# Token and output projections of a two-layer hybrid trunk by three rounded products, with the weights' splits placed among other work, and the parameters in two transfers

## The chip, the cores and the metric

One core of a Trainium2 chip runs the whole program. The metric is the device time of one execution in microseconds, the median of several runs. The core's engines are TensorE (PE, matrix products; PEld is its weight load), VectorE (DVE), ScalarE (ACT), GpSimd (POOL) and SyncE (SP, which issues most transfers). Each has its own queue of instructions and they wait for each other by semaphores.

## The reference

One inference step through two layers, for 128 context tokens and 128 latent tokens of width 1024. Per layer:

```python
ada = silu(cond) @ ada_w + ada_b                 # six vectors of 1024
hm = rms_norm(x) * (1 + sc_m) + sh_m
a_qkv, a_z, a_dec, a_beta, r_qkv, r_g, n_qkv, s_bcx = split(hm @ w_in)
# gated delta rule | retention | neighbourhood attention | gated short convolution
x = x + g_m * (concat(o_gdn, o_ret, o_nat, o_sc) @ w_out)
hf = rms_norm(x) * (1 + sc_f) + sh_f
x = x + g_f * moe(hf)                            # 32 gated-MLP experts, top 1 group, top 2 experts in it
```

## The kernel before

Activations lie transposed: `hT` has 8 tiles of 128 features x 256 tokens (both groups of tokens side by side). The weights stream through a ring of four slots of 6144 columns each, filled by SyncE in a fixed order of loads (16 head slots and 32 experts per layer); a slot is refilled when a semaphore tells that its products are done.

A layer runs in these stages.

1. Opening. `ada` (L414) multiplies the ADA pieces 0 to 2 (load 0 to 2), `ada_rows` (L964, ScalarE) copies each row out, `ada_transpose` (L431, TensorE) turns it, `ada_columns` (L1219, VectorE) adds the bias to it. TensorE issues the transposition of piece i - 1 behind the products of piece i. `modulate` (L955 on ScalarE, L1229 on VectorE) then scales the normalised input.
2. Token projection (L462 to L473): the values of retention and attention and the gates of the delta rule, as plain float32 products, 16 of 512 columns and 16 of 16 columns. The profile shows a plain product as two matmul records.
3. Feature projection (L478): 12 units of 256 weight columns. Here each weight and each input is split into a high half, rounded to the type fp32r, and a low half, the difference; the product is high x high + high x low + low x high (L490, L491, L492). ScalarE makes the high half of a unit (`unit_high`, L979), VectorE the low half (`unit_low`, L1273) in place in the ring. The input's own halves are `ph_hi` (L977) and `h_lo` (L1271). VectorE's queue has the evacuation of the token products (L1253 to L1267) ahead of `h_lo` and of the first `unit_low`.
4. Attention, retention and delta rule. The delta rule runs two chunks (`s` = 0 and 1), each with an inversion by 7 levels (`b` = 0 to 6) for two directions (`g`): GpSimd masks a matrix (L1778), TensorE multiplies (L645), ScalarE copies (L1096), TensorE multiplies again (L666, L670), VectorE adds (L1472, L1474). In chunk 0 pieces of ADA products stand between the levels, in chunk 1 from level 1 on nothing. At the end the state's output (L695) is normed: ScalarE squares (L1100), TensorE sums (L706), ScalarE takes the root (L1103, L1105), VectorE multiplies (L1494, L1496).
5. Output projection (L713 to L726): 8 feature tiles x 8 inputs, 64 plain products of 256 columns, all behind the norm of the delta rule; the residual (L1503) and the sums of squares (L442) follow by parts.
6. Router and experts: 16 pairs, plain float32 products straight from the ring (L818, L867).

The parameters (`param`, 3003 columns: 955 of norms, biases, router and attention bias, then 2048 of cached keys, values and states) come by one transfer (L383), issued behind the layer's first four loads; in layer 1 it also waits until layer 0 is done. VectorE's first instruction of a layer waits for it (L1214, L1215).

## Time and profile before

| | us |
|---|---|
| median of three runs (lowest, highest) | 1288.18 (1279.51, 1291.25) |
| profiled execution | 1287.47 |
| its span | 1285.7 |
| TensorE busy in the span | 1102.2 (86%) |
| VectorE, ScalarE, GpSimd busy | 426.4, 273.8, 86.7 |

The span is what the profile's times refer to (microseconds from its start); the execution's own time has 1.8 us around it. Layer 0 ends near 653 us, layer 1 at the end. PEclk is the granted clock of TensorE as a share of its full speed. In a timeline a row has its start, its length, engine, line, operation, what it writes and reads, how often, and in brackets how long the engine was idle before it and who ended that. Lines are those of the kernel before.

### The profile page before, as it was taken

To read this page: it belongs to the slowest core of one execution; us is meant where nothing else is said; L and a number is where in the kernel's file an instruction comes from. 1 tells how busy PE (TensorE), PEld (TensorE's weight loads), DVE (VectorE), ACT (ScalarE), POOL (GpSimd) and SP (SyncE) were. 2 spreads that over 40 slices of the span, in tenths; PEclk is the share of its full clock that TensorE was granted. 3 is DMA by queue.
4 is the path that set the end of the run, shared out by engine and by line. 5 is a ranking of instruction groups with operands and counts; after the bars stand their busy time and mean duration, and the time that the engine had idled before them with its cause. 6 is when DMAs were issued, how large, how long until landed. Compare 5 with 4: busy or idle time off the path is not lost.

```text
span 1285.7 us, 18039 instructions
## 1 busy us (share of the span) xinstructions
PE 1102.2 (86%) x7588; PEld 781.2 (61%) x7588; DVE 426.4 (33%) x807; ACT 273.8 (21%) x426; POOL 86.7 (7%) x93
## 2 busy tenths in 40 slices
PE   4589877989867999999957996789888699999996
PEld 3379766979664444444354994678877544444443
DVE  0236544444133222222123555353531422222212
ACT  2224441111131111110023445111121211111100
POOL 0000112222000000000000002031310000000000
PEclk9789978999878999999978998799889699999998
DMA  9925630020162999999886256011106179999990
GB/s 391 406 98 197 256 117 34 19 86 2 73 253 97 420 395 412 411 414 410 358 348 281 105 197 263 12 34 38 67 1 253 74 291 407 405 411 413 413 405 36
DMA packets 24412, 299.02 MB, mean 233 GB/s; under 512 B 2944, under 2 KB 2944, under 8 KB 3200
## 3 DMA queue, kind: packets, MB, share of 16 engines
q1 hardware_dynamic: 23904, 296.67, 56.8%
q8 instruction: 66, 1.08, 0.3%
q0 software_dynamic: 416, 1.05, 0.3%
q14 instruction: 26, 0.21, 0.0%
HBM read 295.61 MB, written 2.10 MB: 232 GB/s over the span
## 4 chain that ended last, share of the span: by engine, by line
PE 77%; DVE 7%; issue 6%; ACT 4%; DMA 3%; POOL 1%; SPq 0%; DVEq 0%; POOLq 0%; ACTq 0%
PE ps L818 17%; PE ps L867 9%; PE ps L801 5%; PE ps L829 5%; PE ps L720 5%; PE ps L490 4%; PE ps L492 4%; PE ps L491 4%; PE ps L645 4%; PE ps L670 4%; PE ps L666 3%; DMA param<-in_param 3%; PE ps L466 2%; PE ps L426 2%; POOL arena L1778 1%
## 5 line engine op out<-in xcount | busy, mean ns | idle before, releaser
L818 PE MATMUL ps<-ring,arena 128*64 128x512 f32 x1024 | 226.8, 595 | 1.9 <-DVE arena L1631 1.9
L818 PEld LDWEIGHTS ps<-ring,arena 128*64 128x64 f32 x1024 | 71.6, 137 | 129.5 <-issue 129.1
L490 PE MATMUL ps<-arena_r 128*128 128x256 f32 x384 | 110.9, 289 | 10.4 <-DVE ring_r L1277 10.4
L867 PE MATMUL ps<-ring,arena 128*64 128x512 f32 x512 | 116.9, 598 | 2.0 <-DVE arena L1656 2.0
L492 PE MATMUL ps<-arena_r,ring_r 128*128 128x256 f32 x384 | 111.0, 289 | 0.0
L491 PE MATMUL ps<-hT_r,arena_r 128*128 128x256 f32 x384 | 109.1, 284 | 0.0
L1147 ACT ACTIVATE arena<-ps 128x256 f32<-128x256 f32 (+1 forms) x64 | 31.5, 492 | 244.9 <-PE ps L818 201.4
L426 PE MATMUL ps<-ring,condp 128*32 128x128 f32 x1536 | 57.3, 301 | 28.9 <-DMA ring<-in_ada_w 16.7
L490 PEld LDWEIGHTS ps<-arena_r 128*128 128x128 f32 x384 | 74.8, 195 | 10.6 <-DVE ring_r L1277 10.6
L1147 ACT ACTIVATE arena_r<-ps 128x1024 fp32r<-128x1024 f32 x32 | 32.8, 1024 | 205.9 <-PE ps L867 205.9
L829 PE MATMUL ps<-arena_r 128*128 128x256 f32 x512 | 71.8, 295 | 4.9 <-DVE arena_r L1642 4.9
L491 PEld LDWEIGHTS ps<-hT_r,arena_r 128*128 128x128 f32 x384 | 74.9, 195 | 0.0
L492 PEld LDWEIGHTS ps<-arena_r,ring_r 128*128 128x128 f32 x384 | 74.4, 194 | 0.0
L1277 DVE TENSOR_TENSOR ring_r<-ring,arena_r 128x2048 fp32r<-128x2048 f32 x24 | 54.8, 2291 | 59.1 <-ACT arena_r L987 58.9
L1652 DVE SCALAR_TENSOR_TENSOR arena<-ps,arena 128x256 f32<-128x256 f32 x32 | 15.5, 484 | 174.3 <-ACT arena L1147 174.3
L867 PEld LDWEIGHTS ps<-ring,arena 128*64 128x64 f32 x512 | 34.3, 136 | 60.8 <-issue 56.8
L829 PEld LDWEIGHTS ps<-arena_r 128*128 128x128 f32 x512 | 66.1, 199 | 6.7 <-DVE arena_r L1642 6.7
L1778 POOL TENSOR_TENSOR arena<-arena,const 128x512 f32<-128x512 f32 x56 | 60.5, 1096 | 131.8 <-PE ps L645 72.6
L720 PE MATMUL ps<-hT,ring 128*128 128x256 f32 x256 | 61.0, 403 | 8.5 <-DVE hT L1496 8.5
L426 PEld LDWEIGHTS ps<-ring,condp 128*32 128x32 f32 x1536 | 45.2, 120 | 36.2 <-issue 19.6
L801 PE MATMUL ps<-arena_r,param_r 128*128 128x512 f32 x128 | 56.3, 440 | 11.9 <-DVE hT_r L1668 11.9
L720 PEld LDWEIGHTS ps<-hT,ring 128*128 128x128 f32 x256 | 52.0, 204 | 18.1 <-DVE hT L1496 10.1
(293 smaller groups left out, 1486.8 us busy)
## 6 DMA issues: line engine op xcount, KB each, us to landing
ring<-in_moe SPq DMA_DIRECT2D x64, 2048.0 KB, 10.6
ring<-in_moe SPq DMA_DIRECT2D x64, 1024.0 KB, 10.6
ring<-in_ada_w SPq DMA_DIRECT2D x16, 3072.0 KB, 11.1
ring<-in_w_feat SPq DMA_DIRECT2D x8, 3072.0 KB, 14.0
ring<-in_w_tok SPq DMA_DIRECT2D x2, 2112.0 KB, 27.0
ring<-in_w_out SPq DMA_DIRECT2D x2, 2048.0 KB, 7.3
ring<-in_w_out SPq DMA_DIRECT2D x4, 1024.0 KB, 4.9
param<-in_param SPq DMA_DIRECT2D x2, 1501.5 KB, 25.5
```

The lines of the kernel that those rows point to most:

```text
L426: last = mm(ps[j:j + 32, bank_in, 0:P], condp[:, k, lead:lead + 32], slot[:, k * 768 + m * P:k * 768 + (m + 1) * P], start=u < 4, stop=u > ...
L490: mm(out, hi, ph_hi[:, k, :], start=k == 0, stop=False)
L491: mm(out, hi, h_lo[:, k, :], start=False, stop=False)
L492: last = mm(out, low[:, k, tile], ph_hi[:, k, :], start=False, stop=k == KT - 1)
L720: last = mm(ps[:, f // 2, (f % 2) * TOK:(f % 2 + 1) * TOK], slot[:, at:at + P], hT[:, k, :], start=k == 0, stop=k == KT - 1)
L801: last = mm(bank(bank_out), x[:, s, k * P:(k + 1) * P], sel_r[:, g % 2, s, :], start=n == 0, stop=n == 3)
L818: last = mm(ps[64 * i:64 * i + 64, q % 2, :].rearrange("p (w n) -> p w n", w=2), xg[:, g % 2, k, c0 + 64 * i:c0 + 64 * i + 64], weights[i] ...
L829: last = mm(ps[:, 4 + f // 2, (f % 2) * TOK:(f % 2 + 1) * TOK], y[:, f * P:(f + 1) * P], sel_t[:, q % 2, :], start=q == 0 and f % 2 == 0 a ...
L867: last = mm(ps[64 * i:64 * i + 64, 2 + half, :], act_t[:, q % 2, kk * P + 64 * i:kk * P + 64 * i + 64], ring[(2 * q + i) % RING][:, at:at ...
L1147: go(out, inp, how).then_inc(sem[name], 1)
L1277: tt(tiles768(ring_r[in_load(i) % RING][:], cols), tiles768(ring[in_load(i) % RING][:], cols), pw_hi[v % 2], ALU.subtract).then_inc(sem["p ...
L1778: G.tensor_tensor(group(g, 6), group(g, 2), bc(levels[:, g, b, :].unsqueeze(1), HEADS, P), ALU.mult)\
```

## The change

- The token weights are split as the features' are: ScalarE's high half behind the second ADA row, VectorE's low half behind the second ADA columns. The token weights are loaded ahead of ADA piece 2 for that. The projection is 96 rounded products: high x high in two halves, low x high, high x low.
- VectorE makes the input's low half and the first two units' low halves ahead of the evacuation of the token products.
- The output weights are split in four chunks of 256 columns. ScalarE makes the high halves in levels 2 to 4 of the second inversion and behind it, VectorE the low halves in levels 3 to 5 and behind it. The mixed outputs of retention, attention and convolution are split in levels 1 and 2, those of the delta rule behind its norm.
- The output projection is 192 rounded products. For the first six feature tiles, the products with inputs 2 to 7 stand ahead of the delta rule's norm, those with inputs 0 and 1 behind it; tiles 6 and 7 follow whole.
- The first 955 parameter columns are loaded behind the constants in layer 0, and for layer 1 among the experts of layer 0; the other 2048 stay where the single transfer was.

The diff, cut to its core:

```diff
+TOK_LOAD = 2
 def ada_load(i):
-    return i if i < ADA_FIRST else i + IN_SLOTS
+    return i if i < TOK_LOAD else i + 1 if i < ADA_FIRST else i + IN_SLOTS
 def in_load(i):
-    return ADA_FIRST + i
+    return ADA_FIRST + i if i else TOK_LOAD
...
+                        sp.dma_start(param[:, 0:CACHE], src["param"][l][:, 0:CACHE]).then_inc(sem["param_dma"], 16)
                     if i == RING - 1:
                         if l > 0:
                             sp.wait_ge(sem["layer_done"], l + 1)
-                        sp.dma_start(param[:], src["param"][l]).then_inc(sem["param_dma"], 16)
+                        sp.dma_start(param[:, CACHE:PARAM_W], src["param"][l][:, CACHE:PARAM_W]).then_inc(sem["cache_in"], 16)
                 for q in range(PAIRS):
+                    if q == 2 and l < DEPTH - 1:
+                        sp.wait_ge(sem["flag"], rise(l, "flag", 1))
+                        sp.wait_ge(sem["route_mm"], rise(l, "route_mm", 1))
+                        sp.dma_start(param[:, 0:CACHE], src["param"][l + 1][:, 0:CACHE]).then_inc(sem["param_dma"], 16)
...
+                pe.wait_ge(sem["t_hi"], rise(l, "t_hi", 1))
+                for half in range(2):
+                    pe.wait_ge(sem["h_hi"], rise(l, "h_hi", half + 1))
+                    for part in range(4):
+                        token_products(part, tok_high, ph_hi, True, False, range(4 * half, 4 * half + 4))
+                pe.wait_ge(sem["t_lo"], rise(l, "t_lo", 1))
+                for part in range(4):
+                    token_products(part, tok_low, ph_hi, False, False)
+                pe.wait_ge(sem["h_lo"], rise(l, "h_lo", 1))
+                for part in range(4):
+                    last = token_products(part, tok_high, h_lo, False, True)
...
-                for i, tiles in enumerate(OUT_TILES):
-                    in_slot(l, out_load(i))
-                    for m in range(tiles):
-                        for k in range(KT):
-                            last = mm(ps[:, f // 2, (f % 2) * TOK:(f % 2 + 1) * TOK], slot[:, at:at + P], hT[:, k, :], ...
+                def out_products(f, ks, start, stop):
+                    for n, k in enumerate(ks):
+                        mm(out, high_half(f // 2, k)[:, cols], pm_hi[:, MIX_AT[k], :], ...
+                        mm(out, high_half(f // 2, k)[:, cols], h_lo[:, k, :], ...
+                        last = mm(out, lo[:, k, cols], pm_hi[:, MIX_AT[k], :], ...
+                pe.wait_ge(sem["h_lo"], rise(l, "h_lo", 2))
+                for f in range(6):
+                    pe.wait_ge(sem["p_lo"], rise(l, "p_lo", f // 2 + 13))
+                    out_products(f, range(2, KT), True, False)
+                    if f == 0:
+                        pe.wait_ge(sem["gn_sq"], rise(l, "gn_sq", 1))
+                        mm(bank(7), C("blockones"), group(0, 3).rearrange("p h c -> p (h c)"), start=True, stop=True).then_inc(sem["gn_mm"], 1)
+                pe.wait_ge(sem["h_lo"], rise(l, "h_lo", 3))
+                for f in range(6):
+                    last = out_products(f, range(2), False, True)
+                    if f in (3, 5):
+                        last.then_inc(sem["out_mm"], 1)
+                pe.wait_ge(sem["p_lo"], rise(l, "p_lo", 16))
+                out_products(6, range(KT), True, True)
+                norm_sum(norm2, 2, 5, range(first[0], first[1]))
+                out_products(7, range(KT), True, True).then_inc(sem["out_mm"], 1)
...
                 ada_rows(0, 6)
                 inverse_rms(1)
-                for i in range(1, ADA_FIRST):
-                    ada_rows(i, 6 + i % 2)
+                ada_rows(1, 7)
+                for part, ks in enumerate((slice(0, TOK_K * TOKCOLS), slice(TOK_K * TOKCOLS, KT * TOKCOLS))):
+                    last = go(pt_hi[part].rearrange("p k n -> p (k n)"), ring[n % RING][:, ks], ACT.Copy)
+                last.then_inc(sem["t_hi"], 1)
+                ada_rows(2, 6)
                 modulate(1)
-                go(ph_hi, hT[:], ACT.Copy).then_inc(sem["h_hi"], 1)
+                go(ph_hi[:, 0:4, :], hT[:, 0:4, :], ACT.Copy).then_inc(sem["h_hi"], 1)
+                go(ph_hi[:, 4:KT, :], hT[:, 4:KT, :], ACT.Copy).then_inc(sem["h_hi"], 1)
...
+                        if s == 1 and b in (2, 3, 4):
+                            out_high(b - 2)
+                out_high(3)
...
-                        for i in range(ADA_FIRST):
+                        for i in range(2):
                             ada_columns(i, 5)
+                        dve.wait_ge(sem["t_hi"], rise(l, "t_hi", 1))
+                        for part, ks in enumerate((slice(0, TOK_K * TOKCOLS), slice(TOK_K * TOKCOLS, KT * TOKCOLS))):
+                            last = tt(ring_r[in_load(0) % RING][:, ks], ring[in_load(0) % RING][:, ks], pt_hi[part]..., ALU.subtract)
+                        last.then_inc(sem["t_lo"], 1)
+                        ada_columns(2, 5)
...
+                        if s == 1 and b == 2:
+                            tt(h_lo[:, 2:6, :], hT[:, 2:6, :], pm_hi[:, 0:4, :], ALU.subtract)
+                            tt(h_lo[:, 6:8, :], hT[:, 6:8, :], pm_hi[:, 6:8, :], ALU.subtract).then_inc(sem["h_lo"], 1)
+                        if s == 1 and b in (3, 4, 5):
+                            out_low(b - 3)
```

On VectorE, at the opening of a layer, the kernel before has this order (`adaT` holds the ADA columns, `scale` the modulation's factors):

```order
L1223 TENSOR_TENSOR adaT<-ps,param 128x12 [waits ada_tr]
L1221 REGISTER_ALU
L1223 TENSOR_TENSOR adaT<-ps,param 128x12 [waits ada_tr]
L1227 SCALAR_TENSOR_TENSOR scale<-adaT,param 128x16 [waits ada_dve]
L1243 ISA
L1248 TENSOR_SCALAR hT<-hT,scale,adaT 128x128 [waits h_scaled]
```

and the changed kernel this one, from the second of the three sums on:

```order
L1311 TENSOR_TENSOR adaT<-ps,param 128x12 [waits ada_tr]
L1327 TENSOR_TENSOR ring_r<-ring,arena_r 128x2640 [waits t_hi]
L1327 TENSOR_TENSOR ring_r<-ring,arena_r 128x1584
L1309 REGISTER_ALU
L1311 TENSOR_TENSOR adaT<-ps,param 128x12 [waits ada_tr]
L1315 SCALAR_TENSOR_TENSOR scale<-adaT,param 128x16 [waits ada_dve]
L1337 ISA
L1342 TENSOR_SCALAR hT<-hT,scale,adaT 128x128 [waits h_scaled]
```

The subtraction of the token weights, 2640 and 1584 columns, has moved in between the second and the third sum.

On TensorE, at the end of the delta rule, the kernel before goes from the state's output to the norm's sum and then to the output projection:

```order
L695 MATMUL ps<-arena,param 128x128 x2
L706 MATMUL ps<-arena,const 128x512 [waits gn_sq]
L720 MATMUL ps<-hT,ring 128x256 [waits sc_dve,slot_in1,nat_out,gn_out]
L720 MATMUL ps<-hT,ring 128x256 x31
L720 MATMUL ps<-hT,ring 128x256 [waits slot_in2]
```

In the changed kernel L742 is the state's output; 18 rounded products follow, of which the last three stand here, then the norm's sum (L774) and the next tile:

```order
L763 MATMUL ps<-param_r,arena_r 128x256
L764 MATMUL ps<-hT_r,arena_r 128x256
L765 MATMUL ps<-param_r,ring1_r 128x256
L774 MATMUL ps<-arena,const 128x512 [waits gn_sq]
L763 MATMUL ps<-param_r,arena_r 128x256 [waits p_lo]
```

The norm's sum has 18 products ahead of it, and 90 more stand between it and the first product that waits for the norm.

On VectorE, in the second inversion, an output chunk's low half stands behind the last update of a level (L1583) and ahead of the first of the next (L1581):

```order
L1581 TENSOR_TENSOR arena<-arena,ps 128x512 [waits inv_umm]
L1582 REGISTER_ALU
L1583 TENSOR_TENSOR arena<-arena,ps 128x512 [waits inv_umm]
L1522 REGISTER_ALU
L1525 TENSOR_TENSOR ring1_r<-ring1,arena_r 128x8x256 [waits p_hi]
L1578 REGISTER_ALU
L1580 REGISTER_ALU [waits inv_upd]
L1581 TENSOR_TENSOR arena<-arena,ps 128x512 [waits inv_umm]
```

Before, the same rows stand there without the two in the middle.

## Rows read from the trace of the kernel before

**Rows 1.** The chain that ended last, by engine, from the page

```profile
PE 77%; DVE 7%; issue 6%; ACT 4%; DMA 3%; POOL 1%; SPq 0%; DVEq 0%; POOLq 0%; ACTq 0%
```

**Rows 2.** Groups by line: shapes, count, busy us, mean ns, idle before and its releaser

```profile
L818 PE MATMUL ps<-ring,arena 128*64 128x512 f32 x1024 | 226.8, 595 | 1.9 <-DVE arena L1631 1.9
...
L490 PE MATMUL ps<-arena_r 128*128 128x256 f32 x384 | 110.9, 289 | 10.4 <-DVE ring_r L1277 10.4
...
L1277 DVE TENSOR_TENSOR ring_r<-ring,arena_r 128x2048 fp32r<-128x2048 f32 x24 | 54.8, 2291 | 59.1 <-ACT arena_r L987 58.9
...
L987 ACT ACTIVATE arena_r<-ring 128x2048 fp32r<-128x2048 f32 x24 | 45.6, 1907 | 3.8 <-PE ps L492 3.8
```

**Rows 3.** Stretches: us, busy (x) of PE, PEld, DVE, ACT, POOL, PEclk, DMA share, GB/s

```profile
30.00:44.00 14.00, 4.59 (x98) 4.25 (x97) 0.74 (x2) 0.28 (x1) 0.00 (x0) 0.78 1.01 430
...
76.00:82.00 6.00, 6.00 (x28) 6.00 (x29) 2.10 (x1) 0.00 (x0) 0.00 (x0) 0.50 0.60 258
...
90.00:140.00 50.00, 50.00 (x427) 50.00 (x426) 28.38 (x36) 23.80 (x19) 0.00 (x0) 1.00 0.49 190
...
282.00:292.00 10.00, 8.94 (x51) 8.75 (x52) 3.16 (x5) 1.19 (x2) 3.61 (x4) 0.66 0.45 188
```

**Rows 4.** Timeline of layer 0, opening and token projection

```profile
43.12 0.69 DVE L1215 TENSOR_TENSOR param<-param,const 128x512 f32<-128x512 f32 x1 [42.11 <-DMA param<-in_param]
...
48.12 0.17 DVE L1223 TENSOR_TENSOR adaT<-ps,param 128x12 f32<-128x12 f32 x1 [0.86 <-PE ps L435]
...
48.53 3.18 ACT L961 ACTIVATE hT<-hT,adaT,scale 128x128 f32<-128x128 f32 x8 [1.10 <-DVE scale L1227]
...
51.77 15.51 PE L466 MATMUL ps<-ring,hT 128*128 128x512 f32 x32 [3.69 <-ACT hT L961]
...
75.95 0.58 PE L490 MATMUL ps<-arena_r 128*128 128x256 f32 x1 [5.20 <-DVE ring_r L1277]
```

**Rows 5.** Timeline of layer 1, opening

```profile
659.85 5.35 PE L426 MATMUL ps<-ring,condp 128*32 128x128 f32 x96 [10.68 <-issue]
...
672.35 0.28 ACT L968 ACTIVATE adarow<-ps 128x128 f32<-128x128 f32 x1 [1.03 <-PE ps L435]
...
675.37 0.17 DVE L1223 TENSOR_TENSOR adaT<-ps,param 128x12 f32<-128x12 f32 x1 [1.64 <-PE ps L435]
...
676.60 3.18 ACT L961 ACTIVATE hT<-hT,adaT,scale 128x128 f32<-128x128 f32 x8 [0.90 <-DVE scale L1227]
```

**Rows 6.** Timeline of layer 0, levels 4 and 5 of the second inversion

```profile
302.90 1.95 PE L645 MATMUL ps<-arena 128*128 128x128 f32 x16
...
308.39 1.95 PE L645 MATMUL ps<-arena 128*128 128x128 f32 x16
...
305.91 0.69 DVE L1472 TENSOR_TENSOR arena<-arena,ps 128x512 f32<-128x512 f32 x1 [2.12 <-PE ps L666]
...
309.48 0.60 ACT L1096 ACTIVATE arena<-ps 128x512 f32<-128x512 f32 x1 [4.00 <-PE ps L645]
...
304.04 2.15 POOL L1778 TENSOR_TENSOR arena<-arena,const 128x512 f32<-128x512 f32 x2 [3.35 <-PE ps L645]
```

**Rows 7.** Timeline of VectorE and GpSimd ahead of the second inversion

```profile
276.54 1.16 DVE L1448 TENSOR_TENSOR arena<-arena 128x256 f32<-128x256 f32 x1
...
278.53 0.43 DVE L1448 TENSOR_TENSOR arena<-arena 128x256 f32<-128x256 f32 x1
...
276.33 1.09 POOL L1778 TENSOR_TENSOR arena<-arena,const 128x512 f32<-128x512 f32 x1 [0.70 <-DVE arena L1434]
```

**Rows 8.** Timeline of layer 0, end of the delta rule and output projection

```profile
322.55 0.61 PE L695 MATMUL ps<-arena,param 128*128 128x128 f32 x4
...
329.70 23.45 PE L720 MATMUL ps<-hT,ring 128*128 128x256 f32 x96 [4.24 <-DVE hT L1496]
...
354.72 7.07 PE L720 MATMUL ps<-hT,ring 128*128 128x256 f32 x32
...
328.95 0.69 DVE L1496 TENSOR_TENSOR hT<-arena 128x512 f32<-128x512 f32 x1
```

More of the change, by code:

```diff
@@ L122 @@
 GROUP_W = 8 * 512
+CACHE = PARAM["ck"].start
 PER = dict(
@@ L469, in _, with token_products @@
-                for s in range(NS):
-                    for k in range(KT):
-                        last = mm(ps[:, proj_bank(2), 16 * s:16 * s + 16], hT[:, k, s * P:(s + 1) * P],
-                                  slot[:, k * TOKCOLS:k * TOKCOLS + 16], start=k == 0, stop=k == KT - 1)
-                last.then_inc(sem["proj_mm"], 1)
+                def token_products(part, weight, x, start, stop, ks=range(KT)):
+                    out, cols = ((ps[:, proj_bank(part), 0:16 + TOK], slice(0, 16 + TOK)) if part < 2 else
+                                 (ps[:, proj_bank(2), (part - 2) * TOK:(part - 1) * TOK], slice(16 + TOK, TOKCOLS)))
+                    for k in ks:
+                        last = mm(out, x[:, k, part % 2 * P:(part % 2 + 1) * P], weight(k)[:, cols],
+                                  start=start and k == 0 and part < 3, stop=stop and k == KT - 1, skip_group_check=True)
+                    return last
@@ L1417, in _, with out_low @@
                 copy(qdec.rearrange("p d j (i n) -> p (d j i) n", i=2), bc(gdec[:, 1, :].unsqueeze(2), 8, HD)).then_inc(sem["qd_g"], 1)
+                def out_low(c):
+                    i, part = out_chunk(c)
+                    dve.wait_ge(sem["p_hi"], rise(l, "p_hi", c + 13))
+                    for k0, count, ap in po_hi[c]:
+                        ks = slice(k0, k0 + count)
+                        last = tt(part(ring_r[out_load(i) % RING])[:, ks], part(ring[out_load(i) % RING])[:, ks], ap, ALU.subtract)
+                    last.then_inc(sem["p_lo"], 1)
                 for s in range(NS):
```

138 lines of the change are left out of this document (91 added, 47 removed).

## Prediction

> **What bounds the kernel now.** I read the chain that ended last first, then the lines, then the timeline of the places that the change touches. TensorE makes up 77% of the chain [rows 1]; what it computes, at what clock, and what it waits for is the time. The largest part, the experts, is untouched: TensorE waits there 1.9 us in the whole run for VectorE and not at all for weights [rows 2]. So the gain has to come from the two head stages of each layer.
>
> The clock has to be read with it. A rounded product of 256 columns takes 6.00/28 = 214 ns where the granted clock is 0.50, and 50.00/427 = 117 ns where it is 1.00 [rows 3]. These are the levels of 1.2 and 2.4 GHz.
>
> First place, the token projection: 16 + 16 plain products run from 51.77 us, and only at 75.95 us does the first rounded product of the features start, after 5.20 us of idle time that VectorE's subtractions end [rows 4]. That is 24.2 us; layer 1 has the same two pieces. The idle time is all that L490 shows: 10.4 us in 384 products, 5.2 in each layer [rows 2]. After it the clock is at 0.50 for a window of 6 us, so 28 products cost 28 x (214 - 117) = 2.7 us more. Second place, the output projection: TensorE is done with the state at about 323.1 us (the last row of L695), waits for the norm of the delta rule until 329.70, and the last plain product ends at 361.8 us [rows 8].
>
> **The opening gets longer.** The token weights are now split before the third ADA piece is added up. On ScalarE that is a copy of 4,224 columns: L987 needs 1907 ns for 2048, so 3.93 us. On VectorE it is a subtraction of as many: 2291 ns for 2048, so 4.72 us [rows 2]. Both stand in their engine's queue between ADA piece 1 and ADA piece 2, and the modulation waits for piece 2. VectorE can't begin it early in layer 0, since it first adds piece 1, whose transposition TensorE issues behind the products of piece 2.
>
> Layer 0: VectorE begins at 43.12 us today, when the parameters, the last of the first transfers, have landed [rows 4]. At 430 GB/s [rows 3], the 2048 columns of caches and states (1.05 MB), now last, take 2.4 us, so piece 2 lands at 40.6 us instead of ahead of the token weights. Its 48 products take 5.35 us after a long idle time, as piece 0 does in layer 1 [rows 5], to 46.0; I give the transposition and the sum of piece 1 0.75 us, the subtraction 4.72, and from the sum of piece 2 to the modulation 48.53 - 48.12 = 0.41 [rows 4]. The modulation starts at 51.85 instead of 48.53: 3.3 us late. The shorter wait for parameters is more than used up.
>
> Layer 1: ScalarE copies row 1 at 672.35, and VectorE adds piece 1 at 675.37 [rows 5], so there the split's start is ScalarE's. Its end, 672.6, + 3.93 + 4.72 + gaps and 0.41 gives 681.8 instead of 676.60: 5.2 us late. The parameters landed late in layer 1 too, but what released the modulation there was the sum of piece 2. Together +8.5. The bounds of this term: 0, if the splits cost nothing, and 2 x (3.93 + 4.72) = 17.3, if nothing hides any of them.
>
> **Token products: 11.6 us less per layer.** Removed: 24.2 us and the 2.7 of the low clock. Added: a copy of half of the rounded input (1024 columns, about 1.0 us) before the first product, then 96 products. Half have 256 columns at 117 ns, half 272, in proportion 124 ns: 11.6 us. They now start after the longer idle time at the low clock; I charge the same 2.7 us. No row shows 272 columns; the nearest are 256. If a product of 272 cost nothing more, 0.3 us would go; if all 96 ran at 214 ns, 8.9 would come. Sum 15.3 against 26.9. No wait remains before the features: VectorE's subtraction of the input (2.29) and of the first two weight units (2.29 each) follow one another within 9 us of the modulation, under 14 us of products. What now stands behind these subtractions is the evacuation of the token products; ScalarE's gates wait for it, and behind them the third weight split. I get that split done about 0.8 us before TensorE asks, so it is at the edge; if it comes late, a microsecond or two per layer goes.
>
> **Output products: 13.5 us less per layer.** 192 rounded products at 117 ns are 22.5 us, against 329.70 to 361.8 = 32.1 now [rows 8]. More than half need nothing of the delta rule's norm: 6 feature tiles x 6 inputs x 3 = 108 products, 12.7 us, which fill the wait. From 323.1: 18 products (2.1), the norm's sum (512 plain columns, four pieces at 0.22, 0.9), 90 products (10.5), to 336.6. The norm's chain, ended at 329.6 by L1496 [rows 8], is moved back about 1 us by the first 18 products and gets a copy and a subtraction of 512 columns (a quarter of L987 and of L1277, 0.5 and 0.6): 331.7, so it is hidden by nearly 5 us. Then 36 products (4.2), 24 (2.8), the sum over four tiles (8 pieces at the 0.22 of L720's last row, 1.7 [rows 8]), 24 (2.8): 348.3 against 361.8. The engine comes here at full clock and doesn't stop. The residual and norm behind it are as before.
>
> The splits that make this possible lie in the levels of the second inversion. A level of 5.49 us leaves ScalarE 4.00 us free (copies of 1.9 us fit) and VectorE 2.12 us between the last update and the next level's first [rows 6]. A subtraction of 2.29 overruns by 0.2; an update has 0.2 of slack to the next, so this is made up. The third chunk, in three pieces, overruns by 0.45 at the last level, which nothing makes up: +0.9 in both layers. The fourth lies behind the evacuation of the state, where VectorE waits for the norm anyway.
>
> **A place where the levels can collide.** At 276.54 a VectorE operation with both inputs in SBUF took 1.16 us while GpSimd ran from 276.33 to 277.42; the same line took 0.43 at 278.53, with GpSimd idle [rows 7]. The updates, with one input in PSUM, keep their 0.69 beside GpSimd [rows 6]. The new subtractions are of the kind that was held up. They would start about 0.25 us ahead of GpSimd's pair of masks (304.04), so GpSimd waits some 2 us; its second mask would end near 308.2, and TensorE asks for the first at 308.39.
>
> The Trainium skill (SBUF — State Buffer, section Who interferes with whom) says that the port pair of the two engines is an exclusive lock and that issue order decides who blocks. The trace agrees (1.16 against 0.43 us); by that rule alone it is VectorE that goes first, and the sum above stands unless the order flips.
>
> **Sum.** +8.5 (opening) - 23.2 (token) - 27.0 (output) + 0.9 (levels) = -40.8 us. The profiled execution took 1287.47 us (span 1285.7), 0.7 below the median of 1288.18; I forecast 1287.5 - 40.8 = 1247.
>
> **Rivals.**
> A. GpSimd comes first in the levels. A subtraction waits until 306.2 and ends at 308.5; the second group's update ends three updates later, 310.6, and TensorE wants it at 309.35: 1.25 us in each of four levels and both layers, 10 us: 1257. For it: only 0.25 us decides. Against: VectorE needs no wait before it starts.
> B. Slower than before: the same collision, and the clock falls. After waits of 2.33 us and 0.55 the stretch 282 to 292 ran at 0.66 [rows 3]. If each of five levels had such a wait (2.3) and ran its 5.1 us of products at the half rate, a level would cost 7.4 more: 37 per layer, 74 in all, 1321. It decides from waits of about 2 us per level; rival A's are 1.25, and at 27 us per layer the gain is gone.
> C. The opening costs nothing: the splits end before piece 2 asks, or layer 1 begins sooner with the 955 columns of parameters (0.49 MB) out of its way (TensorE's first product there follows 10.68 us of idle time that no engine ended [rows 5]): 1238. Against: the queues' order.
> D. The splits arrive late, and the output products don't fill the wait: 6.6 of the 13.5 us are lost in each layer: 1260. The change would then do only the half of what it says. For: the third and the fourth chunk end only at 317 and 326. Against: they are asked for at about 332 and 341.
>
> **From cases to numbers.** Forecast 0.71 (1239 to 1256), A 0.10, C 0.10, D 0.06, B 0.03. From 1236 to 1262 holds the forecast, A, C and most of D; above it lie B, the low clock in all token products, and mishaps added up. Faster by over 1% (about what a measurement of this kernel can tell from no change), under 1275: 0.95, all of the cases but B and a bad end of D; within 1%: 0.02; slower: 0.03.
>
> **What would show it.** Token products of some 12 to 15 us and L536 without idle time in front; the modulation at 51.9 and near 681.8; levels that stay near 5.5 us at clock 1.00; the output's last product 25 us after the last product of the state instead of 38.7. Wrong would be: idle time of TensorE that GpSimd or VectorE ends in the second inversion, or waits for weights among the experts.

## The result, and the profile after

The changed kernel took 1242.68 us (median of four runs, 1241.61 to 1245.84) against 1287.89 before (1279.51 to 1291.25): a ratio of 0.966, interval 0.962 to 0.970. Forecast were 1247 and the range 1236 to 1262. The profiled execution took 1242.39 us, its span is 1240.7, so 45.0 us went out of the span where the forecast had 40.8.

The chain that ended last, and the groups by line (columns as in [rows 2]):

```profile
PE 78%; DVE 7%; issue 6%; ACT 4%; DMA 3%; POOL 1%; SPq 0%; DVEq 0%; POOLq 0%; ACTq 0%
```

```profile
L877 PE MATMUL ps<-ring,arena 128*64 128x512 f32 x1024 | 226.8, 595 | 1.9 <-DVE arena L1749 1.9
...
L536 PE MATMUL ps<-arena_r 128*128 128x256 f32 x384 | 107.9, 281 | 0.0
```

TensorE is the bound as before [rows 1], the experts (L877, L818 before) are the same to the tenth, and L536, which is L490 before, has lost its 10.4 us of idle time [rows 2].

The opening and the token projection of layer 0, as a timeline; L1035 and L1327 are ScalarE's and VectorE's halves of the token weights, L1020 the modulation, L498 the token products:

```profile
20.74 0.69 DVE L1303 TENSOR_TENSOR param<-param,const 128x512 f32<-128x512 f32 x1 [19.73 <-DMA param<-in_param]
...
40.51 4.42 PE L460 MATMUL ps<-ring,condp 128*32 128x128 f32 x96 [9.29 <-DMA ring<-in_ada_w]
...
45.37 4.62 DVE L1327 TENSOR_TENSOR ring_r<-ring,arena_r 128x2640 fp32r<-128x2640 f32 x2
...
50.32 3.18 ACT L1020 ACTIVATE hT<-hT,adaT,scale 128x128 f32<-128x128 f32 x8 [4.69 <-DVE scale L1315]
...
54.64 5.43 PE L498 MATMUL ps<-arena_r 128*128 128x272 f32 x32 [8.57 <-ACT arena_r L1040]
59.91 4.04 PE L498 MATMUL ps<-ring_r,arena_r 128*128 128x272 f32 x32
63.78 4.04 PE L498 MATMUL ps<-arena_r,hT_r 128*128 128x272 f32 x32
67.65 0.29 PE L536 MATMUL ps<-arena_r 128*128 128x256 f32 x1
```

ADA piece 2 has landed at 40.51, as worked out (40.6); the modulation starts at 50.32 instead of 48.53 [rows 4], and ScalarE's 4.69 us of idle time in front of it end with the modulation's factors (L1315), which VectorE makes behind the subtraction. The first feature unit follows the token products without a stop, at 67.65 instead of 75.95.

The end of layer 0 and the opening of layer 1, to be held against [rows 5]:

```profile
621.19 2.17 PE L888 MATMUL ps<-arena_r 128*128 128x256 f32 x16 [2.46 <-DVE arena_r L1760]
...
627.66 1.91 ACT L997 ACTIVATE arena<-xT 128x2048 f32<-128x2048 f32 x1 [7.78 <-DVE xT L1621]
...
635.87 5.35 PE L460 MATMUL ps<-ring,condp 128*32 128x128 f32 x96 [12.51 <-issue]
...
648.22 3.81 ACT L1035 ACTIVATE arena_r<-ring 128x2640 fp32r<-128x2640 f32 x2
...
652.06 4.63 DVE L1327 TENSOR_TENSOR ring_r<-ring,arena_r 128x2640 fp32r<-128x2640 f32 x2 [0.83 <-ACT arena_r L1035]
...
657.01 3.18 ACT L1020 ACTIVATE hT<-hT,adaT,scale 128x128 f32<-128x128 f32 x8 [4.82 <-DVE scale L1315]
```

From TensorE's first product to the modulation it is 21.14 us, before 16.75.

The levels of the second inversion (L692 is L645 before, L1896 is L1778, L1525 the output weights' low half, L1587 that of the mixed outputs), to be held against [rows 6, 7]:

```profile
291.89 1.95 PE L692 MATMUL ps<-arena 128*128 128x128 f32 x16
297.38 1.95 PE L692 MATMUL ps<-arena 128*128 128x128 f32 x16
...
288.35 1.58 DVE L1587 TENSOR_TENSOR hT_r<-hT,param_r 128x512 fp32r<-128x512 f32 x1
...
292.70 2.28 DVE L1525 TENSOR_TENSOR ring_r<-ring,arena_r 128x2048 fp32r<-128x2048 f32 x1
...
293.03 3.95 POOL L1896 TENSOR_TENSOR arena<-arena,const 128x512 f32<-128x512 f32 x2 [2.15 <-PE ps L692]
```

A level still takes 5.49 us. VectorE's subtraction began 0.33 us ahead of GpSimd's two masks, took its full speed, 2.28 us, and the masks took 3.95 us instead of 2.15; they ended at 296.98, TensorE asked at 297.38. One level earlier the order did change: the second, short operation of the mixed outputs (L1587) came behind the first of GpSimd's two masks and took 1.58 us, where the same shape takes 0.69 at 320.03 (L1614, below); that level, too, stayed at 5.49 us (286.40 to 291.89).

The granted clock of three stretches (columns as in [rows 3]): the first 32 token products, the start of the second inversion, which stood at 0.66 before, and the levels behind it.

```profile
54.50:60.00 5.50, 5.36 (x33) 5.36 (x34) 4.43 (x3) 4.64 (x4) 0.00 (x0) 0.73 0.14 57
...
271.00:281.00 10.00, 8.94 (x51) 8.76 (x52) 3.15 (x5) 2.66 (x4) 3.59 (x4) 0.66 0.45 188
...
282.00:292.00 10.00, 10.00 (x89) 9.89 (x89) 7.28 (x9) 5.99 (x6) 5.48 (x4) 1.00 0.01 2
```

The second stretch is the one of [rows 3], some 11 us earlier than before; it has the same 51 products and the same 0.66, so the change left it as it was. The levels that the splits went into ran at full clock (1.00 also from 281 to 306.7).

The state's last products (L742), the norm's sum (L774), the low half of the delta rule's outputs (L1614) and the last residual (L1621), in layer 0:

```profile
311.67 0.61 PE L742 MATMUL ps<-arena,param 128*128 128x128 f32 x4
...
314.22 1.02 PE L774 MATMUL ps<-arena,const 128*128 128x512 f32 x2
...
320.03 0.69 DVE L1614 TENSOR_TENSOR hT_r<-hT,param_r 128x512 fp32r<-128x512 f32 x1 [0.70 <-ACT param_r L1207]
...
337.59 1.13 DVE L1621 SCALAR_TENSOR_TENSOR xT<-ps,adaT,xT 128x128 f32<-128x128 f32 x4 [5.62 <-PE ps L765]
```

and the same two places in layer 1:

```profile
919.21 0.61 PE L742 MATMUL ps<-arena,param 128*128 128x128 f32 x4
...
945.17 1.13 DVE L1621 SCALAR_TENSOR_TENSOR xT<-ps,adaT,xT 128x128 f32<-128x128 f32 x4 [5.62 <-PE ps L765]
```

For the sum these rows of the kernel before are needed besides those shown: the last residual of the head in both layers (L1503), the last state product of layer 1, and the end of layer 0.

```profile
361.83 1.12 DVE L1503 SCALAR_TENSOR_TENSOR xT<-ps,adaT,xT 128x128 f32<-128x128 f32 x4 [7.51 <-PE ps L720]
...
950.60 0.61 PE L695 MATMUL ps<-arena,param 128*128 128x128 f32 x4
...
989.88 1.12 DVE L1503 SCALAR_TENSOR_TENSOR xT<-ps,adaT,xT 128x128 f32<-128x128 f32 x4 [7.51 <-PE ps L720]
...
645.61 3.56 PE L829 MATMUL ps<-arena_r 128*128 128x256 f32 x16 [2.46 <-DVE arena_r L1642]
...
653.46 1.91 ACT L938 ACTIVATE arena<-xT 128x2048 f32<-128x2048 f32 x1 [9.17 <-DVE xT L1503]
```

So the 45.0 us divide, each stretch by the difference of its two rows, after less before:

| stretch | forecast, a layer | layer 0 | layer 1 |
|---|---|---|---|
| opening, to the modulation | +3.3, +5.2 | 50.32 - 48.53 = +1.8 | 21.14 - 16.75 = +4.4 |
| modulation to the last state product | -11.6 + 0.45 | 261.35 - 274.02 = -12.7 | 262.20 - 274.00 = -11.8 |
| last state product to the last residual | -13.5 | 25.92 - 39.28 = -13.4 | 25.96 - 39.28 = -13.3 |
| last residual to the end of the layer | 0 | 290.07 - 291.63 = -1.6 | -0.3 |
| end of layer 0 to TensorE's first product | 0 | | 8.21 - 6.39 = +1.8 |

"Modulation" stands for its start (the rows of L1020, and of L961 before), "end of layer 0" for the start of layer 1's first operation on ScalarE (L997, L938 before). The columns add up to -45.1 (the last residual of layer 1 to the end of the span is 295.53 against 295.82).

### The profile page after: what moved, and what is told of

Read it like the earlier page. It is cut to its first block, busy times and chain, and to the rows that moved or that the text cites. A ratio compares the mean times of both kernels' runs of the same rounds, so it can differ in the third digit from the quotient of the medians.

```text
span 1240.7 us, 18440 instructions
## 1 busy us (share of the span) xinstructions
PE 1068.4 (86%) x7780; PEld 773.5 (62%) x7780; DVE 460.0 (37%) x839; ACT 300.6 (24%) x450; POOL 96.2 (8%) x93
## 4 chain that ended last, share of the span: by engine, by line
PE 78%; DVE 7%; issue 6%; ACT 4%; DMA 3%; POOL 1%; SPq 0%; DVEq 0%; POOLq 0%; ACTq 0%
PE ps L877 18%; PE ps L926 9%; PE ps L860 6%; PE ps L888 5%; PE ps L538 4%; PE ps L692 4%; PE ps L536 4%; PE ps L717 4%; PE ps L537 4%; PE ps L713 3%; DMA ring<-in_ada_w 3%; PE ps L498 2%; PE ps L460 2%; POOL arena L1896 1%; PE ps L764 1%
## 5 line engine op out<-in xcount | busy, mean ns | idle before, releaser
L877 PE MATMUL ps<-ring,arena 128*64 128x512 f32 x1024 | 226.8, 595 | 1.9 <-DVE arena L1749 1.9
L877 PEld LDWEIGHTS ps<-ring,arena 128*64 128x64 f32 x1024 | 71.6, 137 | 129.6 <-issue 129.1
L536 PE MATMUL ps<-arena_r 128*128 128x256 f32 x384 | 107.9, 281 | 0.0
L537 PE MATMUL ps<-hT_r,arena_r 128*128 128x256 f32 x384 | 106.6, 278 | 0.0
L460 PE MATMUL ps<-ring,condp 128*32 128x128 f32 x1536 | 57.3, 301 | 35.5 <-DMA ring<-in_ada_w 21.5
L1896 POOL TENSOR_TENSOR arena<-arena,const 128x512 f32<-128x512 f32 x56 | 70.1, 1265 | 126.0 <-PE ps L692 66.7
L1353 DVE TENSOR_TENSOR ring_r<-ring,arena_r 128x2048 fp32r<-128x2048 f32 x24 | 54.8, 2291 | 55.5 <-ACT arena_r L1052 55.3
L888 PE MATMUL ps<-arena_r 128*128 128x256 f32 x512 | 70.3, 291 | 4.9 <-DVE arena_r L1760 4.9
L537 PEld LDWEIGHTS ps<-hT_r,arena_r 128*128 128x128 f32 x384 | 72.1, 188 | 0.0
L536 PEld LDWEIGHTS ps<-arena_r 128*128 128x128 f32 x384 | 72.1, 188 | 0.0
L460 PEld LDWEIGHTS ps<-ring,condp 128*32 128x32 f32 x1536 | 45.3, 121 | 42.6 <-issue 26.5
L538 PEld LDWEIGHTS ps<-arena_r,ring_r 128*128 128x128 f32 x384 | 71.8, 187 | 0.0
L888 PEld LDWEIGHTS ps<-arena_r 128*128 128x128 f32 x512 | 64.6, 195 | 6.7 <-DVE arena_r L1760 6.7
L692 PE MATMUL ps<-arena 128*128 128x128 f32 x384 | 52.5, 291 | 9.4 <-POOL arena L1896 9.4
L1754 DVE TENSOR_REDUCE arena<-ps 64x1 f32<-64x2 f32 x32 | 4.8, 151 | 141.5 <-PE ps L867 141.5
```

The lines of the kernel that those rows point to most:

```text
L460: last = mm(ps[j:j + 32, bank_in, 0:P], condp[:, k, lead:lead + 32], slot[:, k * 768 + m * P:k * 768 + (m + 1) * P], start=u < 4, stop=u > ...
L536: mm(out, hi, ph_hi[:, k, :], start=k == 0, stop=False)
L537: mm(out, hi, h_lo[:, k, :], start=False, stop=False)
L538: last = mm(out, low[:, k, tile], ph_hi[:, k, :], start=False, stop=k == KT - 1)
L692: last = mm(ps[:, 2 + g, h * P:(h + 1) * P], group(g, 6)[:, h, :], group(g, 3)[:, h, :] if b else ident, start=True, stop=True)
L877: last = mm(ps[64 * i:64 * i + 64, q % 2, :].rearrange("p (w n) -> p w n", w=2), xg[:, g % 2, k, c0 + 64 * i:c0 + 64 * i + 64], weights[i] ...
```

## The experiments

Times are medians, beside runs of the kernel before on the same chip (1290.0 for the first four, 1291.2 for the next four, 1289.0 for the last three); the changed kernel was taken along in the last three (e9). Where an edit adds or takes lines, the numbers of the lines behind it shift by a few (L460 is L462 in e10).

**e1, the token projection put back.** Token products plain, their loads behind ADA piece 2 again, no split in the opening, and VectorE's evacuation of the token products again ahead of the input's low half and the first units' low halves:

```diff
-TOK_LOAD = 2
+TOK_LOAD = ADA_FIRST
...
-                    last = token_products(part, tok_high, h_lo, False, True)
+                        last = mm(bank(proj_bank(s)), hT[:, k, s * P:(s + 1) * P],
+                                  slot[:, k * TOKCOLS + 16:(k + 1) * TOKCOLS], start=k == 0, stop=k == KT - 1)
```

> The token projection, its order of loads and the opening are put back as in the kernel before; output projection and the two parameter transfers stay. Theory: the output change is worth -26.8 us (2 x 13.4, as the trace after shows in layer 0). With the parameters early and no split in front of the modulation, layer 0's modulation depends on ADA piece 2 alone: it lands at 34.39 + 1.15 us, its products take 4.45, two transpositions and sums 2.0, so about 42.0 instead of 48.53: -6.5. Layer 1's opening as before. Sum 1287.5 - 26.8 - 6.5 = 1254. Rival: the parameters were hidden anyway (the modulation stays near 48.5): 1260.7. If the token change were the main gain and the output change little (under 5 us per layer): 1270 or more.

Measured: 1254.24, ratio 0.9735 (0.971 to 0.976). The modulation of layer 0, and the first feature unit:

```profile
41.98 3.18 ACT L1008 ACTIVATE hT<-hT,adaT,scale 128x128 f32<-128x128 f32 x8 [0.90 <-DVE scale L1298]
...
70.40 0.58 PE L524 MATMUL ps<-arena_r 128*128 128x256 f32 x1 [5.21 <-DVE ring_r L1349]
```

The modulation comes where the theory has it: at 41.98 without the split in front of it. The wait of 5.21 us before the features is back. So the output change is worth some 27 us, and the early parameters 6.5 us, but only where the opening waits for them. The two make 33.3 of the 35.8 us; the rest is spread over stages between (the largest piece, 2.6 us, from layer 0's modulation to its last state product, 271.38 us instead of 274.02), and its cause stays open.

**e2, the output projection put back.** All of its products plain behind the norm, no splits in the levels:

```diff
-                        if s == 1 and b in (2, 3, 4):
-                            out_high(b - 2)
...
-                        if s == 1 and b in (3, 4, 5):
-                            out_low(b - 3)
...
-                    out_products(f, range(2, KT), True, False)
+                            last = mm(ps[:, f // 2, (f % 2) * TOK:(f % 2 + 1) * TOK], slot[:, at:at + P],
+                                      hT[:, k, :], start=k == 0, stop=k == KT - 1)
```

> The output projection is put back to plain products behind the norm, and no split of output weights or mixed outputs stands in the levels; token projection, opening and parameters stay as changed. Theory: the output's gain is lost and nothing else changes, since the splits in the levels cost nothing: the time after, 1242.5, + 2 x 13.4 = 1269, levels of 5.49 us. Rival (the splits in the levels cost 1.25 us in each of four levels, as in rival A of the prediction): the levels get shorter and the time is 1259.

Measured: 1271.41, ratio 0.9856 (0.984 to 0.987). From the first of the levels' products in question to the state's first product (L730) it takes 25.71 us here (283.69 to 309.40) and 25.84 after (280.91 to 306.75): the splits cost the levels 0.13 us. e1 and e2 together gain 54.4 us (35.8 and 18.6), the whole change 45.2. Most of the difference, 6.5 us, is the parameters', which e1 has and the whole change does not; the rest is within the intervals.

**e3, the parameters last.**

```diff
-                        sp.dma_start(param[:, 0:CACHE], ...)       # behind the constants, and among the experts
                     if i == RING - 1:
+                        sp.dma_start(param[:, 0:CACHE], ...)
                         sp.dma_start(param[:, CACHE:PARAM_W], ...)
```

> The changed kernel, with the first 955 parameter columns put back to the end of the first four loads (behind layer 0 in layer 1). Theory: as long as VectorE's split of the token weights has to wait for the first ADA sums, which TensorE turns behind ADA piece 2, the early parameters hide nothing: ADA piece 2 lands 1.1 us earlier (0.49 MB out of its way), and layer 1 stays: 1241.4, at any rate within 2 us of 1242.5. Rival: the early parameters carry the opening: without them the modulation of layer 0 slips by 3 us or more, 1246 or above, and layer 1's by as much again.

Measured: 1242.91, ratio 0.9637 (0.961 to 0.966), the time of the changed kernel. The parameters are ready at 40.35 us instead of 20.74, and the modulation is no later:

```profile
40.35 0.69 DVE L1299 TENSOR_TENSOR param<-param,const 128x512 f32<-128x512 f32 x1 [39.34 <-DMA param<-in_param]
...
49.67 3.18 ACT L1016 ACTIVATE hT<-hT,adaT,scale 128x128 f32<-128x128 f32 x8 [4.69 <-DVE scale L1311]
```

In the changed kernel the two transfers are worth nothing.

**e4, the low half late.** VectorE's subtraction of the token weights moved:

```diff
                             ada_columns(i, 5)
-                        dve.wait_ge(sem["t_hi"], rise(l, "t_hi", 1))
-                        for part, ks in enumerate(...):
-                            last = tt(ring_r[in_load(0) % RING][:, ks], ..., ALU.subtract)
-                        last.then_inc(sem["t_lo"], 1)
                         ada_columns(2, 5)
                         norm_scale(0, 8, "norm_mix").then_inc(sem["h_scaled"], 1)
...
                 modulate(1)
+                dve.wait_ge(sem["t_hi"], rise(l, "t_hi", 1))
+                for part, ks in enumerate(...):
+                    last = tt(ring_r[in_load(0) % RING][:, ks], ..., ALU.subtract)
+                last.then_inc(sem["t_lo"], 1)
```

> The changed kernel, with VectorE's subtraction of the token weights moved from in front of the third ADA sum to behind the modulation; TensorE first needs it some 5 us after its first token product. Theory (the opening's cost is this subtraction): the modulation starts about 3.9 us earlier in each layer, at 46.4 and 653.1, and no wait takes its place: 1242.5 - 7.8 = 1234.7. Rival: the wait only moves, TensorE stops behind its first 32 token products for the low half (L513) by as much as was won, or for the first feature units: 1242.

Measured: 1237.07, ratio 0.959 (0.957 to 0.961). The modulation comes at 47.67 and 652.16; VectorE subtracts behind it, and TensorE's second group, which needs the low half, follows the first without a stop:

```profile
47.67 3.18 ACT L1020 ACTIVATE hT<-hT,adaT,scale 128x128 f32<-128x128 f32 x8 [0.90 <-DVE scale L1315]
...
49.73 4.62 DVE L1343 TENSOR_TENSOR ring_r<-ring,arena_r 128x2640 fp32r<-128x2640 f32 x2
...
52.00 6.14 PE L498 MATMUL ps<-arena_r 128*128 128x272 f32 x32 [4.78 <-ACT arena_r L1040]
...
57.97 4.06 PE L498 MATMUL ps<-ring_r,arena_r 128*128 128x272 f32 x32
```

No wait took its place. Layer 1 won 3.9 us, as expected (652.16 - 634.96 = 17.2 from TensorE's first product, instead of 21.1), layer 0 2.7; 0.9 of the difference is ADA piece 2, whose products took 5.35 us here and 4.42 in the changed kernel.

**e5, the output behind the norm.**

```diff
-                for f in range(6):
-                    out_products(f, range(2, KT), True, False)
                 pe.wait_ge(sem["gn_sq"], rise(l, "gn_sq", 1))
                 mm(bank(7), C("blockones"), ...).then_inc(sem["gn_mm"], 1)
                 pe.wait_ge(sem["h_lo"], rise(l, "h_lo", 3))
                 for f in range(6):
-                    last = out_products(f, range(2), False, True)
+                    last = out_products(f, range(KT), True, True)
```

> The changed kernel, with the norm's sum ahead of all output products and every feature tile taken whole behind the norm of the delta rule; the splits stay where they are. Theory (108 products fill the wait for the norm): from the end of the state at 312.2 us the norm's chain takes 6.6 as before the change, the copy and subtraction 1.1, then 192 products 22.5 and the sums of squares 1.7: 344.1 instead of 337.55, +6.5 per layer, 1242.5 + 13 = 1255.5, and up to 2.7 more per layer if the granted clock is at 0.50 for a window after the idle time. Rival (the output's gain is the three rounded products alone, and their place gains little): under 1246.

Measured: 1264.41, ratio 0.980 (0.976 to 0.984): some 20 us lost. TensorE's wait for the norm, and the granted clock behind it:

```profile
322.13 0.58 PE L763 MATMUL ps<-param_r,arena_r 128*128 128x256 f32 x1 [5.71 <-DVE hT_r L1610]
```

```profile
320.00:326.00 6.00, 3.87 (x19) 3.88 (x20) 1.30 (x2) 0.63 (x1) 0.00 (x0) 0.53 0.00 0
```

From the last state product (313.51) to the last residual (348.45) layer 0 takes 34.94 us instead of 25.92. Of these 9.0 us 6.9 are idle time (5.71 and 1.18 in front of the norm's sum). Of the 2.1 that are left the low clock is the larger part: the first 15 products, 322.13 to 325.49, took 0.22 us apiece instead of 0.117, 1.6 us in all. In the changed kernel the clock is 1.00 all through this place (312 to 337). So with rounded products in both, the order is worth 9.0 of the 13.4 us that the output gained in a layer, two thirds; the third that is left goes to the rounded products in place of the plain ones. The order with plain products was not tried.

**e6, GpSimd first.**

```diff
                         if s == 1 and b in (3, 4, 5):
+                            if b < 5:
+                                dve.wait_ge(sem["inv_c"], rise(l, "inv_c", 2 * (LEVELS + b + 2) + 1))
                             out_low(b - 3)
```

and the same wait ahead of the mixed outputs at level 2. (`inv_c` counts GpSimd's masks.)

> The changed kernel, with three of VectorE's operations in the levels of the second inversion (the mixed outputs' low half at level 2, the first two chunks at levels 3 and 4) made to wait until GpSimd has its next mask done, so that GpSimd comes first. Theory (the order of issue decides who is held up, as rival A of the prediction priced it): these levels become longer by 1.25 us each, 3 x 2 x 1.25 = 7.5, to 1250; GpSimd's masks are back at 1.1 us. If the second mask holds VectorE up as well, 2 x 1.25: 1257. Rival (the order is of no matter, a level has room for both): levels of 5.49 us and 1242.5.

Measured: 1250.47, ratio 0.969 (0.965 to 0.973). One of the levels:

```profile
295.97 2.28 POOL L1899 TENSOR_TENSOR arena<-arena,const 128x512 f32<-128x512 f32 x2 [3.58 <-PE ps L692]
297.19 3.22 DVE L1525 TENSOR_TENSOR ring_r<-ring,arena_r 128x2048 fp32r<-128x2048 f32 x1 [0.71 <-POOL arena L1899]
...
301.06 2.35 PE L692 MATMUL ps<-arena 128*128 128x128 f32 x16 [0.40 <-DVE arena L1581]
```

With the order turned round it is VectorE that waits (3.22 us for what takes 2.28) and GpSimd that doesn't (2.28 instead of 3.95). From the level at 283.63 to L730 at 312.11 it is 28.48 us instead of 25.84: 2.6 in this layer, 5.3 if the other has the same, of the 7.5 expected; the ratio is 5 us above that of the changed kernel in e9, with intervals of about as much on either side. The Trainium skill (SBUF — State Buffer, section Who interferes with whom) says that a VectorE instruction with two inputs in SBUF contends with a GpSimd instruction that reads SBUF, and that the order of issue decides who blocks; both orders agree, with 3.95 against 2.28 us on GpSimd and 2.28 against 3.22 us on VectorE.

**e7, transfers held, and e10, held until started.** The end of layer 0 brought something that the forecast did not have: TensorE's first product follows 8.2 us behind it instead of 6.4, at the time when the transfers end. Two runs hold the fourth load of layer 1 back:

```diff
+                    if i == RING - 1 and l > 0:
+                        sp.wait_ge(sem["layer_done"], l + 1)                     # e7
+                        sp.wait_ge(sem["ada_row"], rise(l, "ada_row", 1))        # e10
                     ring_in(i, head_slot(l, i))
```

> The changed kernel, with layer 1's fourth load (ADA piece 2, 3 MB) held back until layer 0 is done; the wait for it stood one transfer later, at the cached keys. In every trace so far TensorE's first product of layer 1 follows idle time that no engine ended, 6.4 us (before) to 8.2 us (after) behind the end of layer 0, just when the transfers under way come to their end. Theory (the restart waits for its own instructions, which come behind these transfers): the queues are empty from about 624 to 627.6 us, and TensorE and VectorE start within 3 us of the end of layer 0; ADA piece 2 lands at about 635, ahead of need: 1242.5 - 5 = 1237 or less. Rival (the restart has a length of its own): still 8 us, 1242.5; if ADA piece 2 then comes too late, more.

> The changed kernel, with layer 1's fourth load (ADA piece 2), and the cached keys behind it, held back until ScalarE has copied the first ADA row of layer 1, so that between the token weights' landing (about 624 us) and TensorE's first products of layer 1 no transfer of data runs. In e7_transfers_held VectorE came back 1.8 us behind the end of layer 0 and TensorE, whose restart fell into the next transfers, 7.5 us behind it, with a second stop of 1.96 us. Theory (TensorE's restart, too, waits behind transfers): it starts within 4 us of the end of layer 0 and has no second stop; ADA piece 2 lands 7.2 us after its release, up to 1 us late for its products: 3 us faster than the changed kernel. Rival (TensorE's restart has a length of its own, 12.5 us from its last product): it starts 8 us behind the end of layer 0 again, and the time is the same or up to 2 us longer.

Measured: e7 1245.30, ratio 0.966 (0.962 to 0.971), no gain; e10 1247.88, ratio 0.968 (0.965 to 0.971), beside 0.965 of the changed kernel in e9. In e7, where layer 0 ends at 628.6:

```profile
630.37 0.69 DVE L1303 TENSOR_TENSOR param<-param,const 128x512 f32<-128x512 f32 x1 [1.77 <-issue]
...
636.12 4.04 PE L460 MATMUL ps<-ring,condp 128*32 128x128 f32 x93 [11.79 <-issue]
642.13 0.41 PE L460 MATMUL ps<-ring,condp 128*32 128x128 f32 x3 [1.96 <-issue]
```

VectorE came back in 1.8 us (5.9 in the changed kernel), TensorE in 7.5 (8.2 and, in e9, 8.6 in the changed kernel), and it stopped once more. In e10, where layer 0 ends at 629.8:

```profile
635.51 4.95 PE L462 MATMUL ps<-ring,condp 128*32 128x128 f32 x96 [9.97 <-issue]
...
651.17 5.35 PE L462 MATMUL ps<-ring,condp 128*32 128x128 f32 x96 [3.98 <-DMA ring<-in_ada_w]
```

With nothing else to be moved TensorE came back in 5.7 us, 2.5 sooner than in the changed kernel, and ADA piece 2, which now shared the queues with the cached keys and the next loads, came 4 us late. From 626 to 636 us the DMA queues of e10 show, beside the tail of the token weights, only packets of the kind "instruction":

```profile
q8 instruction: 3, 0.05, 2.9%
q14 instruction: 5, 0.04, 1.4%
```

So in these traces, one of each run, TensorE comes back sooner the less is moved beside it, but most of its restart is its own: neither theory holds alone. VectorE does not follow this: it came back in 1.8 us in e7 and in 3.7 in e10, where less was moved. The Trainium skill (Runtime: NRT & Kernel Launch, section Instruction fetch mechanics) says that a taken branch to a place outside the window at hand has to wait for a fetch by DMA; the packets at this place go with it (the changed kernel has as many there), but what of the 5.7 us they take was not tried and stays open.

**e8, the ADA piece first, and e11, the casts behind.** Both keep the low half late and load ADA piece 2 ahead of the token weights; e8 makes the token weights' high half on two engines ahead of the modulation, e11 all of it on VectorE behind it:

```diff
-TOK_LOAD = 2
+TOK_LOAD = ADA_FIRST
                 ada_rows(2, 6)
+                go(pt_hi[1]..., ring[n % RING][:, TOK_K * TOKCOLS:KT * TOKCOLS], ACT.Copy)      # e8, ScalarE
+                        copy(pt_hi[0]..., ring[nt % RING][:, 0:TOK_K * TOKCOLS])                # e8, VectorE, ahead of ada_columns(2)
                 modulate(1)
+                copy(pt_hi[0]...); copy(pt_hi[1]...)                                            # e11, VectorE
```

> The low half late as in e4_low_half_late, and besides ADA piece 2 loaded ahead of the token weights again, as before the change; the token weights' high half is made behind the third ADA row, 1584 columns by ScalarE and 2640 by VectorE side by side. Theory (with the split's low half out of the way, the opening of layer 0 waits for ADA piece 2, which lands 5 us earlier so): layer 0's modulation starts at 43.5 instead of 47.67 (ScalarE's copy of 1584 columns, about 1.5 us, behind the token weights' landing at 41), layer 1's within 0.5 us of 652.16: 1237.1 - 4 = 1233. Rival (what is won at ADA piece 2 is lost to the copies that now stand in front of the modulation): 1237.

> The changed kernel itself, unchanged, as the measure for the two runs beside it on the same chip: 1242.7 us, 0.966 of the kernel before.

> As e8_ada_piece_first, but all of the token weights' high half is made by VectorE behind its part of the modulation (4224 columns at the 1.54 us for 2640 of that run, 2.5 us), and nothing of it stands in front of the modulation. Theory: the modulation starts at 42.0 (e1_tokens_plain) instead of 43.14 in layer 0, and 1.2 us earlier in layer 1; TensorE's first product follows ScalarE's first half of the rounded input, and the low half is still ahead of need: 1232.1 - 2.4 = 1229.7, 13 us faster than the changed kernel. Rival (VectorE's queue, now 2.5 us longer behind the modulation, comes too late with the low halves, and TensorE stops at its second 32 products or at the first feature units): 1232 or more.

Measured: e8 1232.14, ratio 0.955 (0.951 to 0.959); e11 1231.32, ratio 0.955 (0.952 to 0.958); e9, the changed kernel, 1243.78, ratio 0.965 (0.962 to 0.968). In e8:

```profile
41.28 1.54 DVE L1325 CAST arena_r<-ring 128x2640 fp32r<-128x2640 f32 x1
41.41 1.52 ACT L1035 ACTIVATE arena_r<-ring 128x1584 fp32r<-128x1584 f32 x1
...
43.14 3.19 ACT L1020 ACTIVATE hT<-hT,adaT,scale 128x128 f32<-128x128 f32 x8 [0.21 <-DVE scale L1313]
```

and in e11:

```profile
42.17 3.19 ACT L1020 ACTIVATE hT<-hT,adaT,scale 128x128 f32<-128x128 f32 x8 [0.90 <-DVE scale L1310]
```

The modulation of layer 0 is 7.2 us earlier in e8 than in the changed kernel, and the version is 12 us faster than it. e11 wins another 1.0 us at that place, as expected, but of the 2.4 us forecast 0.8 show in the medians, which is less than these runs can tell. The stop that the rival had did not come: TensorE's second 32 products (52.27) and the first feature unit (60.03) follow without a wait. Either of them beats both kernels of the case.

## Why the prediction was right

**What bounds it.** Right: the experts did not move, and the whole gain lies in the head stages (the two differences at the end of layer 0 come to +0.2 together).

**Opening, +8.5.** The mechanism was right, e4 and e8 show it: VectorE's subtraction stood in front of the modulation, and with it moved away alone the modulations came 2.7 and 3.9 us sooner and the median fell by 5.6 us. The size was 2.3 us too large (+1.8 and +4.4 were measured). The largest part of that is "its 48 products take 5.35 us after a long idle time, as piece 0 does in layer 1": they took 4.42. What they take scatters: behind 8.9 to 9.3 us of idle time they took 4.13 to 5.35 us in the runs with this order of loads (2.83 at full clock, as piece 1), so this part of the miss is chance. The rest is small: 0.45 us instead of 0.75 for the transposition and the sum in layer 0, and in layer 1 8.8 us instead of 9.2 from the start of the split to the modulation, and a start 0.4 us earlier, counted from TensorE's first product. "The shorter wait for parameters is more than used up" was right, and e1 and e3 give its two sides: 6.5 us without the split, nothing with it.

**Token products, -11.6.** Right, a little small: from the end of the modulation (53.50) to the first unit 14.2 us instead of 15.3. The 24.2 us before were 19.0 of plain products and 5.2 of waiting; the 14.2 are 1.1 for the copy and 13.0 of rounded products, and no run takes the two gains apart. The second and the third 32 products took 3.87 us each from start to start, 121 ns apiece, as estimated. The first 32 took 5.27, so the low clock cost 1.4 us and not the 2.7 charged; layer 0 shows 1.4 to 2.8 in the runs with this split, so the charge lay at the top of what occurs and this trace, by chance, at the bottom. "No wait remains before the features" held in every run with the split.

**Output products, -13.5.** Right in both layers (-13.4, -13.3), and the forecast's "25 us after the last product of the state" came out at 25.3 (312.28 to about 337.5). The share of the order was larger than rival D had it: 9.0 us per layer instead of 6.6, since after the wait the clock is low as well (e5).

**Levels, +0.9.** Right that they hide the splits; e2 puts the cost at 0.13 us in layer 0, where 0.45 had been taken for the third chunk's overrun. The price that was set for a flipped order was too high: in e6 a level with a chunk held up took 6.33 us (294.73 to 301.06), 0.84 more than 5.49, where 1.25 had been taken. Where it was priced, at the chunks, the order did not flip.

**Not in the sum.** The end of layer 0 was 1.6 us shorter, since its last products ran at the full clock (2.17 against 3.56 us), and the restart 1.8 us longer. The forecast had neither, but they are not two accidents that cancel. Counted from the start of those last products, TensorE's first product of layer 1 came after 14.2 us before and 14.7 after, and after 14.5 to 15.1 in every other run that holds no transfer back, whether the last products took 2.17 us or over 3.5. What the last products won, the restart waited longer; why is not shown.

**The rivals.** A and B did not occur; e6 shows what A's order costs, and that 0.33 us of order decide it. B's bound, "at 27 us per layer the gain is gone", was wrong: the gain of 40.8 is gone at 20.4 us per layer. C fell with the profile after: the opening cost 6.2 us, and layer 1 began 1.8 us later behind layer 0, not sooner. D fell there too: TensorE stops nowhere between the state and the last product.

## What to carry to other kernels

An operation that prepares data belongs in its engine's queue behind the one that releases the bound engine, as far back as its first consumer allows: the same subtraction held the modulations up by 2.7 and 3.9 us in front of them and made no wait behind them. An early transfer is worth only what the next thing that holds the same operation up leaves of it: the early parameters were worth 6.5 us where nothing else held the modulation (e1), and nothing where the split did (e3). Where products add up into the same sum, take those first whose inputs are ready: it fills the wait and keeps the clock (1.00, against 0.53 in e5's first 6 us), and was worth more here than the cheaper products were.

## What was not expected of the hardware

VectorE makes the rounded copy of 2640 columns in 1.54 us (0.58 ns a column), ScalarE that of 1584 in 1.52 (0.96), while a VectorE subtraction takes 1.12 ns a column (2291 for 2048). The Trainium skill (VectorE: DVE Perf Modes, section Why `tensor_tensor` can't do 2×_2P or 4×) says that an operation with a single source can read two of its elements at once, and one with two tensors can't; the rows agree.

Between the end of layer 0 and TensorE's first product of layer 1, where the outer loop turns, 5.7 to 8.6 us pass in these traces, the least where no transfer runs beside it; ScalarE, which had been waiting for nearly 8 us at that place, starts after 0.03. That is as much as many an edit here was worth.
